# Weight slabs copied inside HBM during attention, and loaded from the copies later

## The reference

```
layer 0:  x += concat(MLA attention, RWKV-7)(rmsnorm(x) @ l0_w_in) @ l0_w_out
          x += peer(rmsnorm(x), l0_peer_wq, keys, u, v)
layer 1:  x += concat(top-k attention, gated MLP)(rmsnorm(x) @ l1_w_in) @ l1_w_out
          x += peer(rmsnorm(x), l1_peer_wq, keys, u, v)

peer(x):  q = x @ w_q                        # 8 heads
          16 best of 128*128 experts per head and token (top-k of two key halves)
          h = gelu(x . u[expert]);  out = sum(gate * h * v[expert])
```

## Time and profile before

| | |
|---|---|
| time, median of 3 runs | 3648.35 us (3647.73 to 3648.91) |
| the profiled execution | 3652.75 us, span 3650.9 us |
| granted TensorE clock | 0.958 of full speed |
| busy share of the span | PE 81%, DVE 71%, POOL 39%, ACT 36% |
| moved by DMA | 1293.40 MB, mean 354 GB/s |

### The profile page before, as it was taken

How to read it: one execution, slowest core, us unless ns; L and a number is a source line. 1 busy time by engine, 2 the same in 40 slices (tenths; PEclk the granted TensorE clock), 3 DMA queues, 4 the chain that set the end, 5 groups by cost and what they waited for, 6 DMA issues and landing times.

```text
span 3650.9 us, 38148 instructions
## 1 busy us (share of the span) xinstructions
PE 2975.2 (81%) x11532; PEld 1418.9 (39%) x11532; DVE 2607.3 (71%) x6403; ACT 1328.6 (36%) x3991; POOL 1407.4 (39%) x1223
## 2 busy tenths in 40 slices
PE   7997877887777777999797878988988867777777
PEld 5774763333223223434344333333434313232222
DVE  2675648876766667798978576999777676667664
ACT  3354213333333333336653232345623323333332
POOL 1200004544434434444345354543444434444443
PEclk9997989999999999999899999998999999999999
DMA  4101039999999999999899999998999999999998
GB/s 133 39 15 47 3 93 417 417 415 421 418 421 415 410 422 402 419 409 375 332 416 396 392 421 419 416 418 335 416 421 421 396 422 421 421 418 410 421 420 350
DMA packets 216573, 1293.40 MB, mean 354 GB/s; under 512 B 23600, under 2 KB 41008, under 8 KB 68784
## 3 DMA queue, kind: packets, MB, share of 16 engines
q0 software_dynamic: 165888, 1208.03, 80.6%
q1 hardware_dynamic: 50480, 82.93, 6.5%
HBM read 1286.49 MB, written 3.87 MB: 353 GB/s over the span
## 4 chain that ended last, share of the span: by engine, by line
DMA 43%; PE 21%; DVE 11%; issue 7%; ACT 3%; POOL 1%; DVEq 0%; ACTq 0%; SPq 0%; POOLq 0%
DMA ring<-in_uv,route 41%; PE banks L1577 16%; DVE ring L1517 4%; DVE X L1527 2%; PE banks L1965 1%; ACT route L1562 1%; PE banks L1905 1%; DVE own L2213 1%; ACT route L1547 1%; POOL ring L1506 1%; PE banks L1931 1%; ACT route L1552 1%; PE banks L2374 0%; DMA own<-in_l_peer_wq 0%; DMA own<-in_l_w_in 0%
## 5 line engine op out<-in xcount | busy, mean ns | idle before, releaser
L1577 PE MATMUL banks<-ring,route 128*128 128x512 f32 (+1 forms) x4088 | 1981.7, 621 | 557.9 <-ACT route L1562 549.0
L1506 POOL DMA_INDIRECT ring<-in_uv,route x1152 | 1320.4, 1146 | 1705.3 <-PE banks L1577 1507.0
L1517 DVE SCALAR_TENSOR_TENSOR ring<-ring,XN 128x1024 f32<-128x1024 f32 x1152 | 1408.8, 1223 | 728.6 <-DMA ring<-in_uv,route 725.9
L1577 PEld LDWEIGHTS banks<-ring,route 128*128 128x128 f32 (+1 forms) x4088 | 724.3, 188 | 1648.7 <-issue 823.3
L1547 ACT ACTIVATE route<-route 128x2 f32<-128x2 f32 x576 | 117.3, 204 | 1855.5 <-DVE ring L1517 1855.2
L1562 ACT ACTIVATE route<-IDN,route 128x128 f32<-128x128 f32 x894 | 309.2, 387 | 3.5 <-PE banks L1577 2.3
L1552 ACT ACTIVATE route<-route 128x1 f32<-128x1 f32 x1152 | 276.7, 287 | 23.5 <-ACT route L1547 0.4
L1905 PE MATMUL banks<-own,QP 128*128 128x512 f32 (+1 forms) x400 | 177.7, 567 | 7.8 <-DMA own<-in_l_w_in 5.4
L1527 DVE SCALAR_TENSOR_TENSOR X<-ring,route,X 128x1024 f32<-128x1024 f32 x130 | 166.5, 1281 | 0.9
L1547 ACT ACT_TABLE_LOAD x106 | 136.0, 1283 | 1.9
L1905 PEld LDWEIGHTS banks<-own,QP 128*128 128x128 f32 x400 | 76.7, 193 | 98.0 <-issue 84.2
(11 more groups left out here) (448 smaller groups left out, 3097.6 us busy)
## 6 DMA issues: line engine op xcount, KB each, us to landing
ring<-in_uv,route POOLq DMA_INDIRECT x1152, 13.1
own<-in_l_w_in SPq DMA_DIRECT2D x16, 1024.0 KB, 16.7
own<-in_l_w_out SPq DMA_DIRECT2D x12, 1024.0 KB, 16.5
own<-in_l_peer_wq SPq DMA_DIRECT2D x12, 1024.0 KB, 16.3
X<-in_x_prompt SPq DMA_DIRECT2D x8, 512.0 KB, 8.4
ring<-in_l_w_in SPq DMA_DIRECT2D x4, 1024.0 KB, 9.8
ring<-in_l_peer_wq SPq DMA_DIRECT2D x2, 2048.0 KB, 12.0
own<-in_l_w_in SPq DMA_DIRECT2D x4, 656.0 KB, 15.5
```

The lines of the kernel that those rows point to most:

```text
L1506: pool.indirect_dma_start(self.ring[:, s % RING, :], None, self.io[f"uv{of_slot(s)[0]}"], bass.IndirectOffsetOnAxis(ap=self.EI[:, g % 2, k ...
L1517: dve.scalar_tensor_tensor(u, u, 1.0, self.XN[:, of_slot(s)[1], :], ALU.mult, ALU.mult, accum_out=self.HD[:, g % 2, k:k + 1]).then_inc(sel ...
L1577: m = pe.matmul(self.bank[1 + half][0:n, :], self.DG[:, (V_TENSOR[s] - 1) % 4, 0:n], self.ring[:, s % RING, D + 512 * half:D + 512 * half ...
```

## The change

A class `Slabs` makes one HBM tensor for each slab, [128, 4, columns], so that the four runs of a partition lie behind each other (8 KB in one piece for 512 columns). `prefetch` issues a copy from HBM to HBM for each of them at its end, during attention. SP waits once, in `tail` ahead of `rest.sp(sp)`, until all copies have landed. The 44 slab loads read the copies; everything else about them (buffers, waits, order) stays. The loads of l0_peer_wq into `WQ` and of l0_w_out in `rwkv`, for the first tile, are as they were.

```diff
+class Slabs:
+    def __init__(self, nc, io, sig):
+        self.io, self.ready, self.n = io, sig("slabs_laid_out"), 0
+        two = [(0, 512), (512, D)]
+        self.parts = dict(l0_w_out=two, l0_peer_wq=two, l1_w_in=COLUMNS, l1_w_out=two, l1_peer_wq=two)
+        self.home = {(name, g, half): nc.dram_tensor(f"slab_{name}_{g}_{half}", (P, HK, b - a), F32).ap()
+                     for name, parts in self.parts.items() for g, (a, b) in enumerate(parts) for half in range(2)}
+
+    def lay_out(self, sp):
+        for name, g, half in self.home:
+            a, b = self.parts[name][g]
+            w = self.io[name].rearrange("(k p) n -> p k n", p=P)
+            sp.dma_start(self.home[name, g, half], w[:, HK * half:HK * half + HK, a:b]).then_inc(self.ready.h, 16)
+
+    def wait(self, sp):
+        sp.wait_ge(self.ready.h, self.ready.at(16 * len(self.home)))
+
+    def load(self, sp, to, name, g, half):
+        return sp.dma_start(to, self.home[name, g, half])
...
             for dst, src in ((W2A[0:64, 0, :], io["b_w2"]), (W2A[64:P, 1, :], io["b_a2"]), (G2[:, :], io["b_g2"])):
                 sp.dma_start(dst, src).then_inc(ll.h, 16)
+
+            slabs.lay_out(sp)
...
-            sp.dma_start(to, w[:, HK * (s % 2):HK * (s % 2) + HK, i:j]).then_inc((self.sl0, self.sl1)[s % 2].h, 16)
+            self.slabs.load(sp, to, name, g, s % 2).then_inc((self.sl0, self.sl1)[s % 2].h, 16)
...
-            w, c = (w_out, s) if s < NO else (w_q, s - NO)
-            sp.dma_start(self.W[s % 2], w[:, HK * (s % 2):HK * (s % 2) + HK, 512 * (c // 2):512 * (c // 2) + 512]
-                         ).then_inc((self.sl0, self.sl1)[s % 2].h, 16)
+            name, c = ("l0_w_out", s) if s < NO else ("l0_peer_wq", s - NO)
+            self.slabs.load(sp, self.W[s % 2], name, c // 2, s % 2).then_inc((self.sl0, self.sl1)[s % 2].h, 16)
...
+            slabs.wait(sp)
             rest.sp(sp)
```

More of the change, by code:

```diff
@@ L51 @@
 SLOTS = 16
+HK = KD // 2
+COLUMNS = [(0, 512), (512, 1024), (1024, CCOLS), (CCOLS, CCOLS + DW), (CCOLS + DW, CCOLS + 2 * DW)]
+class Slabs:
[14 more added lines that the diff above has]
+        return sp.dma_start(to, self.home[name, g, half])
 class Signal:
@@ L319, in encoder @@
         zl, ll = sig("lora_zeroed"), sig("lora_loaded")
+        slabs = Slabs(nc, io, sig)
         def prefetch(sp):
@@ L336, in encoder @@
         lo.close()
-        tail(nc, io, sb, sig, bank, ident, IDN[:, 128:129], X, own, ring, OC, OBT)
+        tail(nc, io, sb, sig, bank, ident, IDN[:, 128:129], X, own, ring, OC, OBT, slabs)
 V_END = KT7 * AH * AV
@@ L1617, in empty @@
         ins.then_inc(self.emptied[at[0]].h, 1)
-COLUMNS = [(0, 512), (512, 1024), (1024, CCOLS), (CCOLS, CCOLS + DW), (CCOLS + DW, CCOLS + 2 * DW)]
 NC, ND, NO, NQ = 6, 4, 4, 4
-HK = KD // 2
 HEADS = [h * 64 for h in range(8)] + [768 + h * 64 for h in range(8)] + [512, 576, 1280]
@@ L1821, in sp @@
         io, nt, b = self.io, self.nt, self.banks
-        w_in = io["l1_w_in"].rearrange("(k p) n -> p k n", p=P)
-        w_out = io["l1_w_out"].rearrange("(k p) n -> p k n", p=P)
-        w_q = io["l1_peer_wq"].rearrange("(k p) n -> p k n", p=P)
         def load(s):
@@ L1828, in load @@
                 self.slab_end(sp, s - 2)
[L1829 to L1832, removed]
-            sp.dma_start(to, w[:, HK * (s % 2):HK * (s % 2) + HK, i:j]).then_inc((self.sl0, self.sl1)[s % 2].h, 16)
+            n = s - NC - ND
+            name, g = ("l1_w_in", s // 2) if n < 0 else ("l1_w_out" if n < NO else "l1_peer_wq", n // 2 % 2)
+            a, z = COLUMNS[g] if n < 0 else (0, 512)
+            to = self.W[s % 2][:, 0:HK * (z - a)].rearrange("p (k n) -> p k n", k=HK)
+            self.slabs.load(sp, to, name, g, s % 2).then_inc((self.sl0, self.sl1)[s % 2].h, 16)
         self.before.finished(sp)
@@ L2337, in sp @@
     def sp(self, sp):
-        w_out = self.io["l0_w_out"].rearrange("(k p) n -> p k n", p=P)
-        w_q = self.io["l0_peer_wq"].rearrange("(k p) n -> p k n", p=P)
         for s in range(NO + NQ):
@@ L2468, in until, with tail @@
             yield m, x[1:]
-def tail(nc, io, sb, sig, bank, ident, half, X, own, ring, OC, OBT):
+def tail(nc, io, sb, sig, bank, ident, half, X, own, ring, OC, OBT, slabs):
     st = ExitStack()
@@ L2513, in tail @@
     for m in mixers:
-        m.half, m.going = half, {}
+        m.half, m.going, m.slabs = half, {}, slabs
     q_pass = {PASSES.index((1, SETS[0][0])): one, PASSES.index((1, SETS[1][0])): two}
```

## The result

The changed kernel takes 3652.18 us (median of 22 runs, 3646.88 to 3657.58), the kernel before 3647.64 us beside it (22 runs, 3643.33 to 3649.80). The ratio is 1.0014, 95% interval [1.0008, 1.0020]: 4.5 us slower, within the 0.2% that the prediction called no change. Forecast were 3684 us and +36 us. The sign was right and the size was not.

The account below looks back on a forecast made before the run. It took `tail` to be bound by the bytes of its 1152 gathers, and earlier blocks by compute chains and barriers. From the median 3648.4 us, +42 for step 2 and -6 for step 1 gave 3684 us, range 3642 to 3724 us.

Parts of the forecast that it names:

- Step 2: The 26 copies in attention: SP, held by a full queue, comes late to the barrier; +42 us, ends 0 and +92.
- I take 210: Copies in attention move at 210 GB/s, so SP is done at 313 us and the next stage starts 41 us late.
- rival B: Copies in attention run at 250 to 352 GB/s, 0 to 25 us late, 3643 to 3668 us; chance 0.13.
- The depth of the queue: SP's issues in attention stand still while about 2600 packets are outstanding, 4.9 copies or 5.1 MB.
- The 1 us for PE's clock after the gap: In the stage behind attention, PE starts at a lower clock after idling; +1 us, ends 0 and 3.
- Step 1: Slab loads from the copies go out in 8 KB pieces; -6 us, ends +5 and -22.
- 3 us for bytes: Slab loads beside the gathers take less DMA time in large pieces; 3 us gained, between nothing and 9.7 us.
- 3 us for waits: PE's 12.1 us of waits for slabs shrink as slabs land sooner; 3 us gained, ends 0 and 12.
- (c): Slab loads can take half the rate for 5 us, delaying two gathers; loss taken as nothing, 5 us as the end.
- D: Slab loads do not come in 8 KB pieces, as views are not merged; step 1 is 0, 3690 us; chance 0.03.
- E: Loads at half the rate let the ring run dry where PE or DVE has no slack; +5 us, 3695 us; chance 0.03.
- likeliest case: Copies in attention at 170 to 250 GB/s, 210 in the middle, D and E inside; 3668 to 3708 us, chance 0.52.

Follow-up runs that it names:

- experiment 1: Changed kernel with its copies kept but unused, the 44 loads reading the original weights in 2 KB pieces: 3661.25 us, ratio 1.0035 to the kernel before.
- experiment 5: Changed kernel with 16 copies issued in attention and the last 10 in the first block of rwkv: 3639.82 us, ratio 0.9976 to the kernel before.
- experiment 8: Changed kernel with every copy made twice, all 52 in attention, tail waiting for both sets: 3734.07 us, ratio 1.0241 to the kernel before.
- experiment 7: Kernel before plus 26 unused copies in attention, from a contiguous source in long pieces, with the old loads: 3646.55 us, ratio 0.9999.
- experiment 3: As experiment 2, with 64 unused columns behind each run so slab loads stay in 2 KB pieces: 3652.54 us, ratio 1.0013 to the kernel before.
- experiment 2: Changed kernel with the last 10 copies moved from attention to the second block of rwkv: 3645.54 us, ratio 0.9992 to the kernel before.
- experiment 4: Changed kernel with only l1_peer_wq copied: 3644.66 us; all but l1_peer_wq copied, copies placed as in experiment 5: 3645.27 us.
- experiment 6: Changed kernel with all 26 copies moved to the second block of rwkv: 3656.24 us, ratio 1.0025 to the kernel before.

## Why the prediction was wrong

**What bounds the kernel** was read rightly: `tail` by its gathers, the blocks ahead of it by chains and barriers.

**Step 2, the mechanism** was right. The copies' bytes are hidden beside attention, the issuing engine is not; it stands still behind a full queue, misses the barrier, and everything behind is moved in full (experiments 1, 5 and 8).

**Step 2, the size** is the term that failed: "I take 210", the rate of a copy from HBM to HBM. It was reached by the thought that read and write share what a load has for one of them. The runs show 322 GB/s in the changed kernel, 326 in experiment 8 and 330 with long pieces. A copy inside HBM loses a quarter of the 421 GB/s of the gathers, not half. That it loses it by reading and writing at once fits, as the length of the pieces makes no difference (experiment 7), but nothing shows it directly. The figure of 207 to 214 GB/s that the Trainium skill gives for tiles of 128 x 16 KiB ("DMA: Bandwidth & Descriptors", latency and other measured facts) does not hold for these copies, and the measurement decides. The prediction's own bounds of 143 to 421 GB/s held the value, and rival B (250 to 352 GB/s, 0 to 25 us late) was what happened, with a chance of 0.13.

**The depth of the queue** was mis-sized in the other direction: 2600 packets outstanding by the count of runs in the front stage, 1570 at the last issue here. What sets the depth stays open: experiment 7 shows that it is not the bytes, and the two counts show that it is not one number of packets either. Both terms corrected, the working of the prediction gives the measured start: (26.5 - 3.1) MB / 322 GB/s = 72.7 us, from 211 us on, is 283.7 us, and SP was done at 283.80. Both terms come from this trace, so this shows only that the sum has no further term. Forecast 41 us late; it was 12.4. Of the 29 us between, the rate is 35 the one way and the depth 6 the other. The 1 us for PE's clock after the gap did not show: the block behind took 57.0 us before, 54.9 after, and 57.0 in experiment 8, behind the longest gap.

**Step 1** was right in sign and near in size: a gain of 6 us forecast, 8.4 to 9.1, 9.0 and 7.0 measured (experiments 1, 5, and 3 against 2). Its parts, 3 us for bytes and 3 us for waits, were not measured apart: experiment 4 splits by loads (3.6 and 3.5 us), its intervals are as wide as the shares, and both halves hold waits. The stretches with slab loads add up to 877 us and not to some 840, which is worth 0.2 us. The prediction did not see the wait for the keys, which takes some 4 us of the gain. That a slab takes half of the rate for 5 us, and that nothing is lost to the gathers behind it (c), both held: the pieces move for about 5 us, and no run with the new loads shows a longer `tail`. D and E are out: 144 packets a slab, and the tail is faster.

**The sum**: +12.4 for SP's lateness and -9 for the loads leave 3.4 us; 4.5 were measured, with an interval from 2.9 to 7.3 us.

**The forecast range** (3642 to 3724 us) held the time, but well below its likeliest case (3668 to 3708 us), and the chances did not hold: 0.73 on a clear loss rested on one rate that no row showed, between bounds that differ by a factor of three.

## What to carry to other kernels

Work that is put beside a stage costs what its issuing engine loses at the next barrier: bytes divided by the measured rate, less what fits into the queue (here 1570 packets of mostly 2 KB), against the slack of that engine in that stage. Put it where both the slack and the neighbours allow it; here a block that had no program for SP at all took the rest of the copies and turned a loss of 4.5 us into a gain of 9.0. When a wait is taken away, look at what the waiting engine needs next, here the keys, and at when that lands. And where a sum hangs on one number that no row shows, and its sign turns inside the bounds, the chances should be spread as wide as the bounds.

## What the runs showed of the hardware that was not expected

- A copy from HBM to HBM moves at 322 to 330 GB/s, whether in 2 KB pieces or in much longer ones.
- A DMA whose source and destination are both contiguous is cut into few long pieces (26.40 MB in 1451 packets with all the rest of the stretch), and SP is free 59 us sooner than with 2 KB pieces, though the bytes move no faster.
- What a load gets beside the gathers, whose pieces are 8 KB, follows the length of its own pieces. A slab of 1.05 MB in 2 KB pieces moved for 11.5 to 13.1 us (80 to 91 GB/s, about a fifth of the whole), in 8 KB pieces for 4.7 to 5.8 us (181 to 223 GB/s, about half), by the packets' own times in the traces of the kernel before and the changed one.
- Copies beside a stage in which PE issues some 3900 matmuls in 185 us make that stage longer: 16.4 us for 26.5 MB in 2 KB pieces, 28.8 us in long ones. Beside attention, with 392 matmuls in 67 us, they cost nothing (experiments 5 and 7). The page of the profile has two queues of instruction traffic (q8, q14), 205 packets in all, and all 21 gaps of PE over 0.7 us end 1.0 to 1.6 us after a 16 KB packet of q8. That the fetch of instructions starts late is shown by this (experiment 6); why it does is not. The gaps grow with the length of the pieces, up to 2.8 us and up to 5.3 us. That fits a fetch that takes its turn with the other rings, as the Trainium skill has it for rings on one DMA engine ("DMA: Bandwidth & Descriptors", queues, rings and completion order: turns at packet granularity). One turn of one piece is enough only for the long ones: at a sixteenth of 322 GB/s a piece of 64 KB takes 3.3 us, but one of 2 KB takes 0.1 us, an estimate from the rate of the copies. With 2 KB pieces something more must wait. Loads in place of copies were not tried.
